# Feed-forward layers of a two-block transformer kernel: all stages of a layer in one program block, and the first low parts of a stage on VectorE

## The reference, cut to what matters

```python
def second_block(x, c, ctx, c_ctx, ...):      # x: 512 tokens, ctx: 256 tokens, D = 1024
    for i in range(2):
        last = i == 1
        mod   = silu(c)    @ ada_w[i] + ada_b[i]      # six parts of 1024: shift, scale, gate, twice
        mod_c = silu(c_ctx) @ ada_w[i] + ada_b[i]     # the same for the context tokens
        h  = modulate(rmsnorm(x, norm_mix_w[i]), sh_m, sc_m)
        hc = modulate(rmsnorm(ctx, norm_mix_w[i]), shc_m, scc_m)
        y, y_c = mixer(h, hc, ...)                    # no y_c in the last layer
        x = x + g_m * y
        x = x + g_f * swiglu(modulate(rmsnorm(x, norm_ffn_w[i]), sh_f, sc_f), w_gate, w_up, w_down)
        if not last:
            ctx = ctx + gc_m * y_c
            ctx = ctx + gc_f * swiglu(modulate(rmsnorm(ctx, norm_ffn_w[i]), shc_f, scc_f), ...)
    return rmsnorm(x, final_norm_w)

def swiglu(h, w_gate, w_up, w_down):                  # hidden width 2816 = 22 slabs of 128
    return (silu(h @ w_gate) * (h @ w_up)) @ w_down
```

## Time and profile before

| | |
|---|---|
| median of 3 runs | 3530.11 us (3527.03 to 3531.21) |
| the profiled execution | 3523.03 us, of it 3521.4 from the first to the last instruction |
| TensorE busy | 2851.1 us, 81% |
| VectorE busy | 1683.2 us, 48% |
| ScalarE busy | 941.0 us, 27% |
| GpSimd busy | 804.5 us, 23% |
| mean granted clock of TensorE | 0.887 of full speed |

### The profile page before, as it was taken

How to read it: one execution, slowest core, us unless ns; L and a number is a source line. 1 busy time by engine, 2 the same in 40 slices (tenths; PEclk the granted TensorE clock), 3 DMA queues, 4 the chain that set the end, 5 groups by cost and what they waited for, 6 DMA issues and landing times. The chain is left out here.

```text
span 3521.4 us, 42052 instructions
## 1 busy us (share of the span) xinstructions
PE 2851.1 (81%) x14724; PEld 2104.8 (60%) x14724; DVE 1683.2 (48%) x3063; ACT 941.0 (27%) x1469; POOL 804.5 (23%) x365
## 2 busy tenths in 40 slices
PE   3997676985996776995996879999996888779997
PEld 2675244333784344333894668787785665667786
DVE  4896642333897643235816654532637224341112
ACT  3224323113224423213216521112112322221112
POOL 1430020111430020210320133222323310143443
PEclk9987886997997886996998989999998988689999
DMA  6530017952530016953511011421414210022222
GB/s 232 195 117 31 1 36 272 346 203 106 190 131 31 1 36 248 342 215 114 205 63 55 25 60 53 139 95 66 149 38 142 67 74 1 30 90 77 101 86 69
DMA packets 92493, 399.08 MB, mean 113 GB/s; under 512 B 16288, under 2 KB 17856, under 8 KB 70976
## 3 DMA queue, kind: packets, MB, share of 16 engines
q1 hardware_dynamic: 63536, 304.47, 24.6%
q0 software_dynamic: 28672, 92.30, 7.2%
q10 hardware_dynamic: 144, 0.52, 0.0%
HBM read 491.09 MB, written 23.59 MB: 146 GB/s over the span
## 5 line engine op out<-in xcount | busy, mean ns | idle before, releaser
L1873 PE MATMUL PS<-one_weights_more,13_h_tokens 128*64 128x512 f32 (+1 forms) x1024 | 230.7, 603 | 2.6 <-ACT 13_h_tokens L1925 1.7
L223 PE MATMUL PS<-one_mix_h_parts,3_w_part 128*128 128x512 f32 x384 | 160.2, 417 | 84.7 <-DVE one_mix_h_parts L438 84.7
L1873 PEld LDWEIGHTS PS<-one_weights_more,13_h_tokens 128*64 128x64 f32 x1024 | 78.2, 139 | 132.8 <-issue 129.0
L224 PE MATMUL PS<-one_mix_h_parts,3_w_part 128*128 128x512 f32 x384 | 153.5, 400 | 0.0
L348 POOL TENSOR_TENSOR 3_w_part<-weights_raw,3_w_part 128x1024 fp32r<-128x1024 f32 x48 | 115.5, 2406 | 104.7 <-ACT 3_w_part L318 104.1
L223 PEld LDWEIGHTS PS<-one_mix_h_parts,3_w_part 128*128 128x128 f32 x384 | 74.4, 194 | 107.8 <-ACT 3_w_part L318 85.5
L348 POOL TENSOR_TENSOR 9_w_part<-weights_raw,9_w_part 128x1024 fp32r<-128x1024 f32 x16 | 42.1, 2637 | 414.6 <-ACT 9_w_part L318 414.6
L1975 DVE SCALAR_TENSOR_TENSOR 13_hid<-13_silu,one_slot_gate,PS 128x256 f32<-128x256 f32 x32 | 15.4, 480 | 226.5 <-ACT 13_silu L1939 226.5
L1896 PE MATMUL PS<-one_weights_more,13_hid_turned 128*64 128x512 f32 (+1 forms) x512 | 117.0, 598 | 2.4 <-ACT 13_hid_turned L1932 2.4
L228 PE MATMUL PS<-one_mix_h_parts,3_w_part 128*128 128x512 f32 x384 | 96.9, 394 | 12.3 <-POOL 3_w_part L348 12.3
L1983 DVE CUSTOM_DVE_ANT_0 13_mod_junk<-weights_raw 128x1024 f32<-128x1024 f32 x64 | 78.3, 1223 | 47.9 <-DMA weights_raw<-in_w_ada 46.8
(11 more groups left out here) (709 smaller groups left out, 7865.9 us busy)
## 6 DMA issues: line engine op xcount, KB each, us to landing
one_weights_more<-in_w_gu SPq DMA_DIRECT2D x128, 1024.0 KB, 10.3
one_weights_more<-in_w_down SPq DMA_DIRECT2D x64, 1024.0 KB, 9.1
weights_raw<-in_f_gu SPq DMA_DIRECT2D x44, 1024.0 KB, 4.9
one_values<-in_w_ada POOLq DMA_DIRECT2D x32, 1024.0 KB, 5.3
weights_raw<-in_w_proj SPq DMA_DIRECT2D x60, 512.0 KB, 3.6
weights_raw<-in_w_ada SPq DMA_DIRECT2D x32, 512.0 KB, 9.8
17_mod_w<-in_w_ada POOLq DMA_DIRECT2D x8, 2048.0 KB, 8.9
2_mod_w<-in_w_ada SPq DMA_DIRECT2D x4, 2048.0 KB, 10.6
```

Source lines behind the costliest of these rows:

```text
L223: nc.tensor.matmul(out, w[0], x[1], start=(j == 0), stop=False)
L224: nc.tensor.matmul(out, w[0], x[0], start=False, stop=False)
L1873: mm = nc.tensor.matmul(M.PS[rows(h), 2 + i % 2, :], h_[:, i % 2, k, rows(h)], weights(i, h, k * 2 * FE), start=(k == 0), stop=(k == KD - 1))
```

## The change

Six edits in one.

1. `gated_up` and `gemm_residual` become classes, `GatedUp` and `GemmResidual`, with one method for each engine, and `run_stages` writes all stages of a layer into one block: each engine goes through the stages in order. There is one `give_all` at the end. Other users of `gemm_residual` get a block with that single stage.
2. The streams of a layer are chained (`before`, `tail`): they share counts, buffers and semaphores, and `base` is the number of chunks before. ScalarE copies the first chunk of the next stage ahead of the last output of this one (`high_of_tail`).
3. The waits at the seams become waits for buffers: the first down chunk multiplies all slabs but the last and then waits for that one (`first`); the first up chunks behind a down stage wait for the PSUM banks that they use (`behind`, `free`). Where a modulation has two conditions, both wait for the whole down stage.
4. In the second and third round the modulation computes one condition (`conds` 1, in PSUM banks 6 and 7); the first round, which makes shift and scale, still has two.
5. With a norm, VectorE makes the low parts of the first two chunks (`first_lows`), behind the norm's ninth product, or behind the last where there are eight tiles. `first_pair` multiplies all high parts of a span of tokens first and then waits for the low ones, chunk by chunk.
6. Buffers are shared: silu's result is multiplied in place, the squares use the same tensor, and the norm's products and the modulation's weights share one.

```diff
 class Stream:
+        if before:
+            before.tail = self
+            self.base = before.base + before.N
+            self.count, self.ready, self.all_parts = before.count, before.ready, before.all_parts
...
+    def wait(self, eng, name, n):
+        eng.wait_ge(self.count[name], n + self.base)
+
+    def load(self, sp, early=None):
+        first = 0 if self.before else 1
+        if early:
+            if self.before:
+                for u in range(2):
+                    self.wait(sp, "split_done", u - 1)
+                    sp.dma_start(self.raw[:, u], self.w(u)).then_inc(self.ready[u], 16)
+            early(sp)
+            first = 1
...
+    def high_of_tail(self, act):
+        if self.tail:
+            self.tail.high(act, 0, 0, 1)
...
         else:
             self.high(act, self.N - 1, 1, self.pairs)
             out(self.N - 2, 0)
+            self.high_of_tail(act)
             out(self.N - 1, 1)
...
+    def first_lows(self, dve):
+        for u in range(2):
+            self.wait(dve, "high_done", u + 1)
+            self.nc.vector.tensor_tensor(self.part[:, u, 1], self.raw[:, u], self.part[:, u, 0].bitcast(F32),
+                                         ALU.subtract).then_inc(self.count["split_done"], 1)
...
     def first_pair(self, pe, terms, spans, done):
-        pe.wait_ge(self.s["high_done"], 2)
-        pe.wait_ge(self.s["split_done"], 2)
+        self.wait(pe, "high_done", 2)
         for a in range(spans):
             for k in range(KD):
                 pe.wait_ge(self.s[done], a * KD + k + 1)
...
+            self.wait(pe, "split_done", 2)
+            for u in range(2):
+                for k in range(KD):
+                    for out, w, x in terms(u, a, k):
                         mm = self.nc.tensor.matmul(out, w[1], x[0], start=False, stop=(k == KD - 1))
-                    if a == spans - 1 and k == KD - 1:
-                        mm.then_inc(self.s["used"], 1)
+                if a == spans - 1:
+                    mm.then_inc(self.count["used"], 1)
...
 class Norm:
-    def multiply(self, dve):
+    def multiply(self, dve, S):
...
             if n:
                 low(n - 1)
+            if n == KD:
+                S.first_lows(dve)
         low(len(self.order) - 1)
+        if len(self.order) == KD:
+            S.first_lows(dve)
...
+class GemmResidual:
+    def sync(self, sp):
+        def early(sp):
+            self.room_free(sp)
+            self.ride.load(sp)
+        self.S.load(sp, early if self.ride else None)
+
+    def free(self, eng, n):
+        if self.ride and (self.ride.conds == 2 or n % 2):
+            n = KD - 1
+        eng.wait_ge(self.s["psum_free"], 2 * self.NS + self.NS * (n + 1))
+
+    def room_free(self, eng):
+        if self.up:
+            self.up.normed(eng)
+            if self.up.down and self.up.down.ride:
+                eng.wait_ge(self.up.down.s["added"], KD)
...
+        def first(n, u, w, low_ready):
+            self.up.free(pe, self.up.NF - 2)
+            self.up.written(pe, KP - 1)
+            products(nc, terms(u, w, range(KP - 1)), low_ready, last=False)
+            self.up.written(pe, KP)
+            for out, pairs in terms(u, w, [KP - 1]):
...
+        def early():
+            if R:
+                if self.up:
+                    self.up.free(act, self.up.NF - 1)
+                R.sigmoid(act)
...
+class GatedUp:
...
+        def behind(n, u, w, low_ready):
+            self.down.free(pe, KD - 2 + u)
+            return products(nc, terms(u, w), low_ready)
...
+        def out(n, u):
+            S.wait(act, "used", n + 3)
+            act.wait_ge(s["low_out"], n + 1)
...
 def feed_forward(nc, M, A, i, spans, rounds, following):
...
+                ride = (modulation(A, 3, per), A["b_ada"][3], A["cond"][1], r * KD * per, per, 1 if r else 2, None,
+                        (weights, shared[:, 4]), 6 if r else 2)
+            last = r + 1 == len(rounds)
+            down = GemmResidual(nc, M, ctx, ffn_down(A, i, f0, NF), hid, spans, 5, 1.0, following if last else None,
+                                ride=ride, stats=last, up=up, room=room)
+            stages += [up, down]
+        run_stages(nc, stages)
```

More of the change, by code:

```diff
@@ L227, in products @@
         for j, (w, x) in enumerate(pairs):
-            mm = nc.tensor.matmul(out, w[1], x[0], start=False, stop=(j == len(pairs) - 1))
+            mm = nc.tensor.matmul(out, w[1], x[0], start=False, stop=(last and j == len(pairs) - 1))
     return mm
@@ L315, in high @@
     def high(self, act, n, u, loads):
-        act.wait_ge(self.ready[u], 16 * loads)
-        act.wait_ge(self.s["used"], n + 1)
-        self.nc.scalar.activation(self.part[:, u, 0], self.raw[:, u], ACT.Copy).then_inc(self.s["high_done"], 1)
+        act.wait_ge(self.ready[u], 16 * (loads + self.base // 2))
+        self.wait(act, "used", n + 1)
+        self.nc.scalar.activation(self.part[:, u, 0], self.raw[:, u],
+                                  ACT.Copy).then_inc(self.count["high_done"], 1)
@@ L320, in highs @@
+    def high_of_tail(self, act):
+        if self.tail:
+            self.tail.high(act, 0, 0, 1)
     def highs(self, act, out, early=None, both=False):
-        self.high(act, 0, 0, 1)
+        if not self.before:
+            self.high(act, 0, 0, 1)
         if both:
@@ L1291, in _, with run_stages @@
+def run_stages(nc, stages):
+    with nc.Block() as block:
         @block.sync
         def _(sp):
-            if ride:
-                R.load(sp)
-            S.load(sp)
+            for st in stages:
+                st.sync(sp)
+        @block.gpsimd
+        def _(pool):
+            for st in stages:
+                st.gpsimd(pool)
         @block.tensor
         def _(pe):
-            def chunk(n, u, w, low_ready):
-                pe.wait_ge(s["psum_free"], NS * n + NS)
-                terms = [(M.PS[:, 4 * u + a, 0:nt], [(blocks(w, k), tokens(src, k, t0, nt)) for k in range(KP)])
-                         for a, (t0, nt, _) in enumerate(spans)]
-                return products(nc, terms, low_ready)
@@ L1305, in _ @@
-            S.open(pe)
-            if mix is not None:
-                pe.wait_ge(s["h_done"], KD)
-            S.multiply(pe, chunk)
-            if not stats:
-                return
-            sums.add_gathered(pe)
-            sums.spread(pe)
-        @block.gpsimd
-        def _(pool):
-            if ride:
-                R.load_first(pool)
-            if not stats:
-                S.lows(pool, R.load_next if ride else None)
-                return
-            for n in range(KD):
-                S.low(pool, n, n % 2)
-                if ride and n >= 2:
-                    R.load_next(pool, n // 2, n % 2)
-                if n >= 4:
-                    sums.gather(pool, n - 3)
-            for k in (KD - 3, KD - 2):
-                sums.gather(pool, k)
+            for st in stages:
+                st.tensor(pe)
@@ L1330, in _ @@
         @block.scalar
         def _(act):
-            if mix is not None:
-                for k in range(KD):
-                    nc.scalar.activation(src[:, 0, k], mix[:, k, :], ACT.Copy).then_inc(s["h_high"], 1)
-            if not stats:
-                S.highs(act, lambda n, u: None, (lambda: R.sigmoid(act)) if ride else None)
-                return
-            def square(k):
-                act.wait_ge(s["scaled"], NS * (k + 2))
-                sums.square(act, k)
-            for n in range(KD):
-                S.high(act, n, n % 2, n // 2 + 1)
-                if ride and n == 0:
-                    R.sigmoid(act)
-                if n >= 2:
-                    square(n - 2)
@@ L1387, in adopt, with gemm_residual @@
+def gemm_residual(nc, M, *args, **more):
+    with ExitStack() as ctx:
+        run_stages(nc, [GemmResidual(nc, M, ctx, *args, **more)])
 def adopt(nc, M, plus_one):
@@ L2227, in _ @@
                 R.load_first(pool)
-                S.lows(pool, R.load_next, rides // 2, 1)
+                S.lows(pool, R.load_next, rides // 2, 1, not norm)
             else:
-                S.lows(pool)
+                S.lows(pool, first=not norm)
         @block.vector
@@ L2234, in _ @@
             if norm:
[L2235 removed]
+                H.multiply(dve, S)
             if ride:
```

374 lines of the change are left out of this document (229 added, 145 removed).

## The result

The changed kernel takes 3423.73 us (median of 4 runs, 3419.81 to 3430.18) against 3530.25 (4 runs, 3527.03 to 3531.21) for the kernel before. The ratio is 0.9702, with a 95% interval of 0.9684 to 0.972. That is 106.5 us less by the medians, where 94.2 had been worked out (3436). The two profiled executions have spans of 3521.4 and 3419.2 us, 102.2 apart.

A forecast was written before the change was run, and what follows sets the result against it. TensorE bounds the stages; gains lie mainly between them. Savings of 20.5 + 20.9 + 5.5 + 11.2 + 9.4 + 26.7 = 94.2 us from 3530.1 give 3436; own range 3427 to 3446, over cases 3420 to 3461.

The forecast's parts named there:

- The norm's start: Four stages beginning with a norm: low parts move to VectorE and TensorE starts on high parts alone; 20.5 us saved.
- the upper bound of 4.8: Norm's start: VectorE's low parts of 2048 elements cost at most GpSimd's own 4.8 us; then some 7 us less gained.
- Layer 1's seams: Layer 1's three feed-forward seams cost nothing any more, and the stages' excess over matmul time goes; 20.9 us saved.
- First down stage: Layer 0, both conditions still computed: everything moves up, but GpSimd's next low parts hold VectorE; 5.5 us saved.
- the 10.2 less 5.5 of the prediction: Layer 0's first down stage: saving of 10.2 us without GpSimd holding VectorE, against 5.5 with it.
- Second down stage: Layer 0, one condition only: both seams and the stages' excess go; 11.2 and 9.4 us saved.
- Last down stage: Layer 0, last up matmul to last residual addition: 59.0 us instead of 85.7, at 7.6 a chunk; 26.7 us saved.
- VectorE keeps up: Rival for layer 0's first and last down stages: holds fall between VectorE's instructions; 105 us saved, 3425; chance 0.2.
- The seams stay in part: Rival at the eight seams: entering loops or new code costs issue time; 24 us lost, 3460; chance 0.22.
- The clock falls in a long run: Rival in layer 0's feed-forward: granted clock drops to 1.2 GHz during long matmul work; slower, 3646; chance 0.03.
- The merged buffers re-create the barrier: Rival at the seams: waits for merged buffers act as the barrier, only norm and fewer reductions count; 3490; chance 0.05.

The follow-up runs named there:

- the two experiments that come near to these signs: Changed kernel with GpSimd's next low parts after VectorE's last readout, 3421.37 us; changed kernel with squares one chunk later in last down stages, 3421.63 us.
- the best variant: Changed kernel with GpSimd's next low parts later in layer 0 and squares one chunk later in last down stages: 3403.26 us, ratio 0.9654.

## Why the prediction was right

By its own steps, the changed trace against that of before. *The norm's start*: 3.2 + 8.5 + 1.2 + 8.5 = 21.4, predicted 20.5 (2.5, 8.3, 1.4, 8.3). VectorE's subtraction of 2048 elements took 2.28 us and not 2.6, well under the upper bound of 4.8; TensorE's first product in layer 0 came 7.1 us sooner (a wait of 7.3 for 14.4), as predicted. *Layer 1's seams*: 21.5, predicted 20.9; no wait is left. *First down stage*: 5.8, predicted 5.5. The wait inside it is 2.5 (predicted 3.5), the one behind it 7.8 (about 8), the second activation comes 8.7 us after the matmuls' end (9.9), and the next up stage starts 79.0 after it (79.2). The last two figures agree by luck in part: the activation came 1.2 us sooner than forecast, and 1.0 of that was lost again. It may have gone where no run looked: the prediction had each chunk's own low part over in time, but already in the trace of before three of the stage's eight additions are held by them (0.75 to 1.33 us instead of 0.16), and in the changed one those of the third to the sixth chunk take 1.25 to 1.33. The hold by the next stage's low parts that I had assumed fell where I had put it, and taking it away gave back 4.7, which is the 10.2 less 5.5 of the prediction. *Second down stage*: 21.2, predicted 11.2 + 9.4. *Last down stage*: 28.2, predicted 26.7. From the last SiLU's start to the end of the last addition it is 57.6 instead of 59.0: the first addition ended at 11.1 and not 11.6, and the seven behind it took 46.5 and not 47.4. The long periods were 7.37, three of them, where 7.9 and three times 7.6 had been put.

These make 98.1 of the span's 102.2. The rest was no step of mine: 3.0 in blocks 18 to 21, in which the trace of before had been longer than those of other kernels with the same code, and 1.1 spread over all else. The medians are 4.3 further apart than the spans, which is scatter of the runs. So of the 12.3 us by which the forecast missed, 3.9 belong to its own terms and 8.4 to nothing that it had a term for; without these the time would lie in the forecast's own range. The mechanisms were right, and each of the five terms was between 0.3 and 1.5 too small. Three sizes were off for a reason. The start of the down stages was priced with the barrier's order (product, table load, activation in series behind the last product), while the changed ScalarE loads its table at 2210.01, right behind the SiLU; this is also why the wait inside the first down stage is 1.0 shorter. The low parts were a tenth cheaper. And one trace of before was taken for all of them.

Of the rivals, *VectorE keeps up* (3425) names the measured time better than mine, by luck: its two signs, no wait after the first down stage and a period of 6.3, are absent, and the two experiments that come near to these signs shorten their stages by 4.7 and 2.4. *The seams stay in part* falls with the waits and with stages of 65.5 = 8 x 8.18. The Trainium skill (Runtime: NRT & Kernel Launch, Instruction fetch mechanics) would have a taken branch out of the loaded pages wait for a fetch. No run here shows such a wait at the written-out chunks. *The clock falls in a long run*: with the seams closed the granted clock is 0.98 to 1.00 in every stage shown above. *The merged buffers re-create the barrier*: excluded by 54.8 us of merging, with one wait of 7.8 left at eight seams.

On the hold itself the Trainium skill (SBUF — State Buffer, SBUF: two separate sides) goes further than what the prediction used: whichever of the two starts first keeps the shared ports for its whole instruction, and the other is fully blocked. The trace agrees: 4.34 us for four elements, ended with the low part. L1145, which has one SBUF input beside PSUM, keeps its 1.22 us each of the 24 times that it runs beside GpSimd's work for 0.3 us or more in the changed trace.

One count of the recorded text is wrong and costs nothing. A chunk of an up stage has 48 matmuls for 512 tokens (x480 for ten chunks in the earlier trace rows), 32 with high weights and 16 with low ones, not 96; in layer 0 the 256 context tokens add 48. So 0.1748 us is the mean over matmuls of both widths, a pair takes twice that, and a down chunk with 8 slabs has 24 pairs. The chunk times of the prediction, 8.39, 6.29, 8.18 and 6.82, come out the same.

## What to carry to other kernels

When barriers go, look for whoever was idle behind them: here GpSimd's work for the next stage moved into a stretch in which VectorE was the last to finish, and held it. Early work of an engine that holds another is only worth starting when its result is due; a single wait on it won 4.7 us. A wait in the list is no price: the 2.5 us for a weight copy could be removed, and the stage became 1.4 us longer.

## What the runs showed that I had not expected

A cast with one SBUF input is held as well as those with two: 2.65 us (and 2.66 in the changed kernel at 2409.34) instead of 0.56 beside a low part. The trace of before has it too: its cast L2120 takes 3.83 us at 2130.15, to 2133.98, beside two low parts of GpSimd that run from 2123.63 to 2133.56.

The same stretch of matmuls, blocks 32 to 34, took between 167.4 and 190.5 us in thirteen profiled runs of kernels that do not differ there, at granted clocks of 0.80, 0.70 and 0.67 in the three shown. This scatter of 23 us is three times the best variant's gain over the changed kernel, so that gain is shown by stage lengths alone. What decides the clock there is open: it was not tried.
